# Ten pairs of expert tiles in V's second half multiplied with seven block products each

## What is computed

```python
u = u_emb[expert]
a = gelu(einsum('thkd,td->thk', u, xb))      # U: 256 tokens x 16384 experts
coef = g * a
out = einsum('thk,thkd->td', coef, v_emb[expert])   # V: coef (256 x 16384) times v (16384 x 2048)
x = x + out
return rmsnorm(x, norm_final_g)
```

## Time and profile before

| | us |
|---|---|
| median of three runs | 3175.64 |
| profiled execution, whole | 3175.95 |
| its span, first to last instruction | 3174.1 |
| TensorE busy | 3160.3 (100% of the span) |
| VectorE busy | 2096.0 (66%) |
| ScalarE busy | 1804.0 (57%) |
| GpSimd busy | 458.0 (14%) |
| granted TensorE clock, mean | 0.999 |
| DMA, mean rate | 198 GB/s |

### The profile page before, as it was taken

One profiled execution on the slowest core, in us unless ns is written; L12 is line 12 of the kernel. 1 busy time (PEld: TensorE's weight loads), 2 busy tenths in 40 slices (PEclk: granted clock), 3 DMA queues, 4 the chain that ended last, 5 costly groups with the idle time before them and its releaser, 6 DMA issues.

```text
span 3174.1 us, 58774 instructions
## 1 busy us (share of the span) xinstructions
PE 3160.3 (100%) x24186; PEld 3018.3 (95%) x24186; DVE 2096.0 (66%) x3389; ACT 1804.0 (57%) x2580; POOL 458.0 (14%) x321
## 2 busy tenths in 40 slices
PE   9999999999999999999999999999999999999998
PEld 9999999999999999999999999999999888888887
DVE  7987486666664477665666699855555666666665
ACT  6566464444444455545455578877777544555545
POOL 0001200000000000000000056777760000000000
PEclk9999999999999999999999999999999999999999
DMA  6444557666666656545565577888876777766555
GB/s 224 151 146 134 183 181 235 225 226 229 226 201 194 194 172 206 163 153 166 187 196 197 199 190 194 196 195 195 194 195 196 243 242 242 242 226 216 195 194 168
DMA packets 229419, 627.77 MB, mean 198 GB/s; under 512 B 59328, under 2 KB 78624, under 8 KB 229024
## 3 DMA queue, kind: packets, MB, share of 16 engines
q1 hardware_dynamic: 192144, 623.60, 60.7%
q0 software_dynamic: 36864, 0.15, 3.3%
q10 hardware_dynamic: 144, 0.26, 0.0%
HBM read 601.27 MB, written 21.10 MB: 196 GB/s over the span
## 4 chain that ended last, share of the span: by engine, by line
PE 98%; DVE 1%; ACT 0%; DMA 0%; issue 0%; POOL 0%; SPq 0%; DVEq 0%; ACTq 0%; POOLq 0%
PE ps L941 32%; PE ps L942 31%; PE ps L943 31%; PE ps L1014 0%; DVE wl L1481 0%; PE ps L1215 0%; PE ps L1238 0%; PE ps L1235 0%; PE ps L982 0%; DMA raw<-in_in1k 0%; PE ps L1411 0%; PE ps L1249 0%; PE ps L1239 0%; PE ps L1067 0%; PE ps L1016 0%
## 5 line engine op out<-in xcount | busy, mean ns | idle before, releaser
L2273 ACT CAST wh<-raw 128x1024 fp32r<-128x1024 f32 (+3 forms) x1114 | 1158.2, 1040 | 1029.7 <-PE ps L943 1008.4
L1481 DVE TENSOR_TENSOR wl<-raw,wh 128x1024 fp32r<-128x1024 f32 (+2 forms) x883 | 1061.8, 1203 | 407.8 <-ACT wh L2273 405.4
L941 PE MATMUL ps<-xh,wh 128*128 128x256 f32 x3088 | 854.7, 277 | 0.5 <-issue 0.5
L943 PE MATMUL ps<-xh,wl 128*128 128x256 f32 x3088 | 850.0, 275 | 0.0
L942 PE MATMUL ps<-xl,wh 128*128 128x256 f32 x3088 | 849.8, 275 | 0.0
L941 PE MATMUL ps<-xw,wh 128*128 128x258 f32 (+2 forms) x2096 | 591.7, 282 | 2.8 <-DVE wl L1542 1.7
L943 PE MATMUL ps<-xw,wl 128*128 128x258 f32 (+2 forms) x2096 | 587.6, 280 | 0.0
L941 PEld LDWEIGHTS ps<-xh,wh 128*128 128x128 f32 x3088 | 579.7, 188 | 4.3 <-issue 1.6
L942 PEld LDWEIGHTS ps<-xl,wh 128*128 128x128 f32 x3088 | 579.8, 188 | 1.1 <-issue 1.0
L943 PEld LDWEIGHTS ps<-xh,wl 128*128 128x128 f32 x3088 | 579.6, 188 | 0.0
L2784 POOL DMA_INDIRECT table<-w_loose x256 | 397.6, 1553 | 809.3 <-DVE w_loose L2161 656.3
(11 more groups left out here) (398 smaller groups left out, 4454.7 us busy)
## 6 DMA issues: line engine op xcount, KB each, us to landing
raw<-in_peer_u SPq DMA_DIRECT2D x256, 512.0 KB
raw<-in_peer_v SPq DMA_DIRECT2D x256, 512.0 KB
raw<-in_w_in SPq DMA_DIRECT2D x172, 512.0 KB
raw<-in_w_up SPq DMA_DIRECT2D x82, 512.0 KB
raw<-in_w_gate SPq DMA_DIRECT2D x80, 512.0 KB
raw<-in_w_down SPq DMA_DIRECT2D x80, 512.0 KB
raw<-in_w_out SPq DMA_DIRECT2D x64, 512.0 KB
table<-tmp SPq DMA_DIRECT2D x32, 512.0 KB, 6.4
```

Of the source, the lines that this page charges most:

```text
L941: t.matmul(o, lh, rh, start=start, stop=False)
L943: return t.matmul(o, ll, rh, start=False, stop=stop)
L1481: v.tensor_tensor(part_at(wl, i), raw[:, i % RN, 0:cols(i)], high.bitcast(F32), ALU.subtract).then_inc(lo, 1)
L2273: last = s.copy(part_at(wh, i), raw[:, i % RN, 0:cols(i)])
```

## The change

In V's second half ten pairs of tiles (24 and 25, 34 and 35, ... 114 and 115) leave the list of chunks. A pair is a product of 2 x 2 blocks: coefficients A (two token halves x two tiles) times weights B (two tiles x two column halves). It is computed by Winograd's form of Strassen's scheme, with seven block products in place of eight. The sums of blocks that this needs are made by GpSimd: four of weights (128x512) and four of coefficients (128x128).

- **Loads.** SyncE loads a pair's two tiles into `pair_raw`, which is the memory of the low half of the old activations, behind TensorE's use of the pair before (PAIR_LOAD, 8 chunks ahead).
- **GpSimd** makes the eight sums in place (pair_sums).
- **ScalarE** casts four quarters of 128x1024 to `pair_high`, one in each of loops j - 5 to j - 2, where j is the pair's first tile (pair_step with o = 3 to 6). Each waits for GpSimd's sums.
- **VectorE** subtracts four quarters of 128x1024 in loops j - 4 to j - 1 (pair_step with o = 4 to 7), after that loop's own coef_low and cut.
- **TensorE** (v_pair, between tiles j - 1 and j + 2) waits for all four low quarters, then makes 21 matmuls of 128x512. Three of the products stay in PSUM banks 0 to 3; the four shared ones gather over all ten pairs in banks 4 to 7.
- **The fold.** After the last pair ScalarE copies one bank and VectorE makes eight adds of 128x512 in loops 117 to 124 (FOLD), which bring the gathered products into the residual.
- **Banks 4 to 7** must be free by the first pair, so the additions of the first half move to loops 11 to 14, the squares and the gain to loops 52 to 83, and the residual's pieces are loaded from tile 8 on. `fin` is laid out anew to suit that.

```diff
-PLAN += [("V", j, c) for c in range(2) for j in range(128)]
+PAIRS = [24 + 10 * n for n in range(10)]
+PAIRED = [j + e for j in PAIRS for e in range(2)]
+SINGLE = [j for j in range(128) if j not in PAIRED]
+PLAN += [("V", j, 0) for j in range(128)] + [("V", j, 1) for j in SINGLE]
...
-PIECE = {AT["V", 10 + 2 * n, 1]: n for n in range(12)}
-
-ADD_AT = [50 + 4 * n for n in range(4)]
...
+ADD_AT = [11, 12, 13, 14]
+SQUARE_AT, GAIN_AT = [52, 62, 72, 82], [53, 63, 73, 83]
...
+PAIR_LOAD = {AT["V", PAIRS[0] - 4, 1]: 0}
+PAIR_LOAD.update({AT["V", j + 2, 1] + 6: n + 1 for n, j in enumerate(PAIRS[:-1])})
+BEHIND_PAIR = {j - 8 + o: (n, o) for n, j in enumerate(PAIRS) for o in range(8)}
+FOLD = {PAIRS[-1] + 3 + n: n for n in range(8)}
...
+            if i in PAIR_LOAD:
+                n = PAIR_LOAD[i]
+                if n == 0:
+                    y.wait_ge(gemm, AT["U", 127, 1] + 1)
+                for e in range(2):
+                    if n:
+                        y.wait_ge(pair_mm, PAIR_MM + 3 * (n - 1) + 1 + e)
+                    j = PAIRS[n] + e
+                    y.dma_start(pair_raw[:, CH * e:CH * e + CH], A["peer_v_2"][128 * j:128 * j + 128, CH:2 * CH]).then_inc(d_pair, 16)
...
+        def v_pair(n):
+            j = PAIRS[n]
+            one, two = 128 + j, 128 + j + 1
+            first, last = n == 0, n == len(PAIRS) - 1
+
+            def product(o, left, b, start, stop):
+                return three(o[:], *left, pair_block(pair_high, b), pair_block(pair_low, b), start, stop)
+
+            def single(tile, qt):
+                tk = slice(128 * qt, 128 * qt + 128)
+                return coef_at(0, tile)[:, tk], coef_at(1, tile)[:, tk]
+
+            def summed(i):
+                return pair_sum_at(pair_high, i), pair_sum_at(pair_low, i)
+
+            if first:
+                t.wait_ge(f_add, 4)
+            t.wait_ge(pair_lo, PAIR_LO + 4 * (n + 1))
+            t.wait_ge(c_l, one + 1)
+            product(ps[4], single(one, 0), B11, first, last)
+            product(ps[5], summed(0), T1_, first, last)
+            t.wait_ge(c_l, two + 1)
+            product(acc(1, 0, 0), single(two, 0), B21, False, False)
+            product(acc(1, 1, 0), single(two, 1), T4_, False, False).then_inc(pair_mm, 1)
+            product(acc(1, 0, 1), summed(3), B22, False, False).then_inc(pair_mm, 1)
+            product(ps[6], summed(1), T2_, first, last)
+            product(ps[7], summed(2), T3_, first, last).then_inc(pair_mm, 1)
...
+                if c and j - 2 in PAIRS:
+                    v_pair(PAIRS.index(j - 2))
...
+        def pair_step(n, o):
+            if o >= 4:
+                q = slice(CH * (o - 4), CH * (o - 4) + CH)
+                v.wait_ge(pair_hi, PAIR_HI + 4 * n + o - 3)
+                v.tensor_tensor(pair_low[:, q], pair_raw[:, q], pair_high[:, q].bitcast(F32), ALU.subtract).then_inc(pair_lo, 1)
...
+            steps = [(folded, ps[4]), (fin_at(0, CH + 512), folded), (fin_at(0, CH + 512), ps[5]), (folded, ps[7]),
+                     (fin_at(1, CH), folded), (fin_at(1, CH + 512), folded), (fin_at(1, CH + 512), ps[5]), (fin_at(0, CH), ps[4])]
+            x, y = steps[n]
+            if n == 0:
+                v.wait_ge(pair_hi, PAIR_HI + 4 * len(PAIRS) + 1)
+            else:
+                v.wait_ge(pair_sum, PAIR_SUM + 8 * len(PAIRS) + n)
+            v.tensor_tensor(x, x, y if y is folded else y[:], ALU.add).then_inc(pair_sum, 1)
...
+            if j in PAIRS:
+                coef_low(128 + j + 1)
+                cut(AT["V", j + 2, 1] + 2)
+                continue
...
+            elif j in SINGLE and j - 2 not in PAIRS:
+                cut(AT["V", j, 1] + 2)
+            if j in BEHIND_PAIR:
+                pair_step(*BEHIND_PAIR[j])
+            if j in FOLD:
+                fold(FOLD[j])
...
+            elif n >= 130 and n - 130 in PAIRED:
+                s.wait_ge(pair_mm, PAIR_MM + 3 * (PAIRED.index(n - 130) // 2) + 1)
...
+        def pair_step(n, o):
+            if 3 <= o < 7:
+                q = slice(CH * (o - 3), CH * (o - 3) + CH)
+                s.wait_ge(pair_sum, PAIR_SUM + 8 * n + (3, 4, 4, 8)[o - 3])
+                if o == 4:
+                    s.wait_ge(d_pair, D_PAIR + 32 * (n + 1))
+                if n:
+                    s.wait_ge(pair_mm, PAIR_MM + 3 * n)
+                s.copy(pair_high[:, q], pair_raw[:, q]).then_inc(pair_hi, 1)
...
+        def pair_sums(n):
+            j = PAIRS[n]
+            g.wait_ge(coef, j + 2)
+            a11, a21, a12, a22 = [G[:, j + e, 128 * qt:128 * qt + 128] for e in range(2) for qt in range(2)]
+            raw_at = {b: pair_block(pair_raw, b) for b in range(7)}
+            sums = [pair_sum_at(pair_raw, i) for i in range(4)]
+            done = PAIR_SUM + 8 * n
+            if n:
+                g.wait_ge(pair_mm, PAIR_MM + 3 * n)
+            g.wait_ge(d_pair, D_PAIR + 32 * (n + 1))
+            g.tensor_tensor(raw_at[T3_], raw_at[B22], raw_at[T1_], ALU.subtract).then_inc(pair_sum, 1)
+            g.tensor_tensor(raw_at[T1_], raw_at[T1_], raw_at[B11], ALU.subtract).then_inc(pair_sum, 1)
+            g.wait_ge(pair_sum, done + 2)
+            g.tensor_tensor(raw_at[T2_], raw_at[B22], raw_at[T1_], ALU.subtract).then_inc(pair_sum, 1)
+            g.wait_ge(pair_sum, done + 3)
+            g.tensor_tensor(raw_at[T4_], raw_at[B21], raw_at[T2_], ALU.subtract).then_inc(pair_sum, 1)
+            g.tensor_tensor(sums[0], a21, a22, ALU.add).then_inc(pair_sum, 1)
+            g.wait_ge(pair_sum, done + 5)
+            g.tensor_tensor(sums[1], sums[0], a11, ALU.subtract).then_inc(pair_sum, 1)
+            g.tensor_tensor(sums[2], a11, a21, ALU.subtract).then_inc(pair_sum, 1)
+            g.wait_ge(pair_sum, done + 6)
+            g.tensor_tensor(sums[3], a12, sums[1], ALU.subtract).then_inc(pair_sum, 1)
...
```

More of the change, by code:

```diff
@@ L167 @@
 V1 = AT["V", 0, 1]
[L169 to L171 removed]
+PIECE = {AT["V", j, 1]: n for n, j in enumerate((8, 10, 12, 14, 16, 18, 20, 22, 26, 28, 30, 32))}
+ADD_AT = [11, 12, 13, 14]
[4 more added lines that the diff above has]
+FOLD = {PAIRS[-1] + 3 + n: n for n in range(8)}
 UEND = [AT["U", j, 1] - U0 for j in range(128)]
@@ L678, in in_heads, with fin_at, pair_block, pair_sum_at @@
         return x.rearrange("p (h s) -> p h s", h=8)
-    fin = flatG[:, 0:2 * D].rearrange("p (q d) -> p q d", q=2)
+    def fin_at(qt, c, n=512):
+        o = 2 * CH * (c // CH) + CH * qt + c % CH
+        return flatG[:, o:o + n]
+    pair_high, pair_low = [x[:, PAD_X[3]:PAD_X[3] + KT * S] for x in xbuf]
+    pair_raw = x_loose[:, 1, PAD_X[3]:PAD_X[3] + KT * S]
+    B11, T1_, B21, B22, T3_, T2_, T4_, SUMS = range(8)
+    folded = flatG[:, 3 * D + 3 * CH:3 * D + 3 * CH + 512]
+    def pair_block(x, b):
+        return x[:, 512 * b:512 * b + 512]
+    def pair_sum_at(x, n):
+        return x[:, 512 * SUMS + 128 * n:512 * SUMS + 128 * n + 128]
     gain = flatG[:, 2 * D:3 * D]
@@ L933, in _ @@
                     y.wait_ge(sem, 2 * qt + n + 1)
-                    y.dma_start(out[128 * qt:128 * qt + 128, c:c + 512], fin[:, qt, c:c + 512]).then_inc(d_out, 16)
+                    y.dma_start(out[128 * qt:128 * qt + 128, c:c + 512], fin_at(qt, c)).then_inc(d_out, 16)
         y.wait_ge(d_out, 8 * 16)
@@ L2670, in square_up @@
             s.wait_ge(f_add, n + 1)
-            s.activation(squares[:, qt, 512 * i:512 * i + 512], fin[:, qt, 512 * i:512 * i + 512], ACT.Square,
+            s.activation(squares[:, qt, 512 * i:512 * i + 512], fin_at(qt, 512 * i), ACT.Square,
                          accum_out=ssum[:, qt, i:i + 1]).then_inc(f_sq, 1)
+        def pair_step(n, o):
[7 more added lines that the diff above has]
+                s.copy(pair_high[:, q], pair_raw[:, q]).then_inc(pair_hi, 1)
         for j in range(128):
+            if j in PAIRS:
+                coef_high(128 + j + 1)
+                cut(AT["V", j + 2, 1] + 2)
+                continue
             if j < 126:
@@ L2684, in _ @@
                 s.copy(part_at(wh, i)[:, 512:CH], raw[:, i % RN, 512:CH]).then_inc(hi, 1)
-            else:
+            elif j in SINGLE and j - 2 not in PAIRS:
                 cut(AT["V", j, 1] + 2)
-            if j - 1 in ADD_AT:
-                n = ADD_AT.index(j - 1)
+            if j in BEHIND_PAIR:
+                pair_step(*BEHIND_PAIR[j])
+            if j == PAIRS[-1] + 2:
+                s.wait_ge(pair_mm, PAIR_MM + 3 * len(PAIRS))
+                s.copy(folded, ps[6][:]).then_inc(pair_hi, 1)
+            if j in SQUARE_AT:
+                n = SQUARE_AT.index(j)
                 square_up(0, n // 2, n % 2)
@@ L2708, in _ @@
                 s.wait_ge(f_out, 4)
-                s.dma_start(out[128:256, 512:1024], fin[:, 1, 512:1024]).then_inc(d_out, 16)
+                s.dma_start(out[128:256, 512:1024], fin_at(1, 512)).then_inc(d_out, 16)
     @block.gpsimd
@@ L2805, in _ @@
         put(1, 7)
+        def pair_sums(n):
[20 more added lines that the diff above has]
```

(3 more changed lines are left out.)

28 lines of the change are left out of this document (15 added, 13 removed).

## The result

The changed kernel takes 3196.73 us, the kernel before 3175.6 in the same rounds: a ratio of 1.0067 [1.0049, 1.0084], 21.1 us slower, where 12.6 were forecast.

A forecast was written before the change was run, and what follows sets the result against it. TensorE was taken as the bound, busy 3160.3 of 3174.1 us. The span, 3174.1 - 6.8 (matmuls) + 14 (stalls) + 0.8 (squares) + 4.5 (GpSimd turns) = 3186.6, became 3188.2 us after adjustments; range 3180 to 3206.

The forecast's parts named there:

- Sign: Whole kernel: slower than the kernel before, chance 0.80; same 0.12, faster 0.08.
- The quarter behind the cut: Ahead of each pair: VectorE's last quarter queues behind the cut and stalls TensorE 1.4 us, 14 us for ten.
- Rival (a): Ahead of pairs: the last quarter costs nothing, VectorE being 35% idle; full gain, 3168.8 us, chance 0.08.
- Turns with GpSimd: Between pairs: VectorE and GpSimd alternate on SBUF, delaying coefficients 0 to 0.9 us per pair, 4.5 us in all.
- The squares: Pairs 54, 64, 74 and 84: ScalarE's square delays the last cut and quarter some 0.2 us each, 0.8 us.
- The gain's product behind the quarter: Loops 53 to 83: VectorE's gain products follow the last quarter; coef_low ends at 5.0 of 5.4 us, no cost.
- GpSimd's deadline: GpSimd starts about 9 us after a pair's first matmul; sums done at 12.5 to 15, needed at 14.4, just in time.
- Rival (c): Between pairs: GpSimd's sums too late, holding ScalarE and the coefficients; 3201 to 3210 us, half of it 3195, chance 0.16.
- SyncE, fold, moved additions: Load queue, loops 11 to 14 and 117 to 124: later loads and VectorE's added adds are hidden, no cost.
- The clock: TensorE's new 1.4 us gaps leave the granted clock at 1.00, no cost.
- The new ones have the same shape, so I give them the same 0.227: Pairs on TensorE: 21 matmuls replace 24 at 0.227 us each, saving at most 6.8 us for ten pairs.
- my forecast proper: Whole kernel: stalls of 1.1 to 1.6 us and contention of 0 to 0.9 per pair give 3181 to 3193, chance 0.66.

The follow-up runs named there:

- e2: The changed kernel with GpSimd filling its eight sums per pair with constants instead of adding (output not the reference's): 3189.29 us, ratio 1.0045 to the kernel before.
- e1: The changed kernel with VectorE making the pair's quarter ahead of the loop's usual cut instead of behind it: 3190.61 us.
- e3: The changed kernel with both edits, quarter ahead of the cut and constants in place of GpSimd's sums (output not the reference's): 3177.51 us.
- e6: The changed kernel with eight pairs twelve tiles apart, quarter before cut, helper work moved or reordered to give room, another product order: 3177.75 us.
- e5: The kernel before with an added TensorE wait for the next tile's low coefficients at eleven tiles (10, 20, ... 110) of V's second half: 3196.44 us.
- e12: The kernel before with three probes: met waits (tile 20), another PSUM bank (66), moving operand in the pairs' memory (84); outputs of 66, 84 wrong: 3178.22 us.
- e4: The kernel before with one added TensorE wait for tile 11's low coefficients ahead of tile 10 of V's second half: 3185.43 us.
- e8: e6 with ScalarE's and VectorE's quarters one tile earlier: 3177.78 us.
- e9: The kernel before with a wait for tile 11's low coefficients after six matmuls of tile 10, met 0.07 us ahead of the next weight load: 3175.84 us.
- e11: The kernel before with a wait for ScalarE's cast of chunk 12 after nine matmuls of tile 10, expected about 0.25 us early: 3175.07 us.

## Why the prediction was right, and where it was not

- **Sign and main mechanism: right.** The quarter behind the cut was to cost 1.4 us ahead of each pair; it costs 1.38 where nothing else is late, and e2 leaves ten stalls of 1.32 to 1.41 (13.5 us for 14 forecast). Rival (a), VectorE's idle time gives the room, falls with the list at tile 34, in which VectorE has no idle time. In e2, where no backlog is left, it has 0.10 us in each of these loops, in front of the cut, as said.
- **Turns with GpSimd: right in kind.** 4.5 us forecast for the middle, 4.6 measured. I had let the small adds end the backlog in time; in four pairs it reached the quarter, 2 us more. The Trainium skill (SBUF — State Buffer, section "SBUF: two separate sides") says that VectorE with two SBUF inputs and a GpSimd instruction that reads SBUF lock each other out for a whole instruction. This trace agrees: 2.32 us for a cut of 1.23, and 2.15 for GpSimd's next add.
- **The squares** were to cost 0.8 us and cost next to nothing: in e2 the stalls of the four pairs that have one (54 to 84) are 1.34 to 1.35, those of the others 1.32 to 1.41. In the changed kernel three of these four pairs have long stalls, but so has pair 104, and e2 takes them all away. The gain's product behind the quarter was rightly said to be hidden here; once the pairs start earlier it is not (0.69 us in e1, 0.27 in e3, four times each).
- **GpSimd's deadline: right.** It started 9.0 us behind the first pair's first matmul (2892.81 - 2883.82) and 8.3 to 9.8 behind the others', where 9 was put, and ScalarE waited for it 2.1 us in all, which coefficients had to spare. Rival (c) fell.
- **SyncE, fold, moved additions:** no wait of TensorE names them. The clock: 1.00, as said.
- **The step that failed** is the one sentence "The new ones have the same shape, so I give them the same 0.227", and with it the silent assumption that the old ones keep it. Shape and clock did stay the same; the pitch of all the matmuls that follow, some 1170 of them in tiles that the change never touches, went to 0.2333. That is 7.5 us, and with 2.0 more for GpSimd's backlog and 0.9 less for squares and stalls it is the 8.5 us between 12.6 and 21.1. The measured 3196.73 lies in my range by luck: the range reached to 3206 for another reason, rival (c), which did not happen, and my forecast proper ended at 3193. That end was also added up wrongly: 3175.64 - 6.8 + 16 + 0.8 + 9 is 3194.6, which still lies below the measurement.
- **The rows of before could have warned me.** There the last thirty matmuls or so, from 3158.6 us, are 0.2333 apart, behind the late weight load in tile 125. I had read one tile and taken its pitch for the engine's.

**Would it pay if the helpers were never late?** No: e6 has no hold-up at all and is level with the kernel before, since the longer pitch (7.7 us) takes more than eight or ten pairs give (5.4 or 6.8). None of these versions is faster than the kernel before. A version whose pair operands lie in the memory of the usual `wh` and `wl` buffers might keep the short pitch; it was not tried.

**What stays open:** why there are two pitches, what keeps one for 118 tiles, why every third hold-up of e5 turned it back, what happens in tile 125, and which property of the operand's place it is in e12 (distance, alignment or the buffer's last writer). The place alone does not make matmuls slow: in the kernel before, U's matmuls of 128x256 from 2021 to 2469 us all have their moving operand in this same memory (`xh`, `xl`) and start 0.1133 us apart, half of the shorter pitch. Shown is only that some events turn it and others do not.

## What to carry to other kernels

A method that saves matmuls has to be charged with two things that the matmul count doesn't show: the last helper instruction of its preparation, if it queues behind the usual one on a nearly full engine (1.38 us each time here), and what it does to the pitch of all matmuls behind it. Before TensorE's time is called fixed, measure the distance of starts, to 0.001 us over a whole stretch, on both sides of every wait: 3% of the pitch over 1400 matmuls was worth more here than the removed work. And an engine that is 65% busy on average has no room in the loops that matter, if its work there is 2.62 us of 2.72.

## What the runs showed of the hardware that I had not expected

- Matmuls of 128x512, each with its weight load, start 0.2267 or 0.2333 us apart, both at a granted clock of 1.00. Between turns the pitch keeps its value, in e4 for 118 tiles.
- It turned long at a hold-up of 1.3 us (e4) and at eight of eleven (e5; at the other three it was short behind them), and without a hold-up at three matmuls with the moving operand in another buffer (e12). It also turned, in either direction and without a hold-up, at a weight load in tile 125 that started 0.01 to 0.05 us behind the matmul before it, where others start 0.003 to 0.004 behind (the kernel before, e5, e6, e8, e12). Two more met waits or another PSUM bank did not turn it (e12), nor did added waits that were met in time by 0.07 us or more (e9 to e11).
- VectorE and GpSimd, each with two operands in SBUF, take turns one by one when both are queued: cut 1.23 to 2.32 us, coef_low 0.43 to 1.51, GpSimd's add of 128x512 1.36 to 2.15. Eight adds of GpSimd so took 10.4 to 12.2 us.
- Ten gaps of 1.3 to 2.0 us on TensorE, one in some 29 us, left its granted clock at 1.00 in V's second half.
